# Both squared-ReLU MLPs of a two-layer decoder trunk, 29 of 32 weight tiles a layer multiplied by one level of Strassen's scheme

## The reference

```python
def mlp(h, w_up, w_down):                 # D_MODEL = 1024, D_FF = 4096
    u = jax.nn.relu(h @ w_up)
    return (u * u) @ w_down
# x = x + mlp(rmsnorm(x, w), w_up, w_down)   for each of the two layers
```

## Time and profile before

| | |
|---|---|
| median of three runs | 2374.9 us (2372.99 to 2383.7) |
| profiled execution, first to last instruction (span) | 2389.7 us |
| PE busy | 2199.2 us, 92% |
| DVE busy | 1364.9 us, 57% |
| ACT busy | 754.3 us, 32% |
| POOL busy | 396.1 us, 17% |
| MLP 0, MLP 1 | about 801 to 1186 us and 1984 to 2373 us |

### The profile page before, as it was taken

How to read it: one execution, slowest core, us unless ns; L and a number is a source line. 1 busy time by engine, 2 the same in 40 slices (tenths; PEclk the granted TensorE clock), 3 DMA queues, 4 the chain that set the end, 5 groups by cost and what they waited for, 6 DMA issues and landing times.

```text
span 2389.7 us, 41891 instructions
## 1 busy us (share of the span) xinstructions
PE 2199.2 (92%) x17594; PEld 2071.3 (87%) x17594; DVE 1364.9 (57%) x2086; ACT 754.3 (32%) x1439; POOL 396.1 (17%) x267
## 2 busy tenths in 40 slices
PE   7998897888899999999998998999899879999998
PEld 7988776777789999999998987897798759999997
DVE  4886776856654635344565564664656647353443
ACT  4332334445443312122313322322332334122221
POOL 1000101101121100000045443244325500000000
PEclk9999998887999999999999999999999989999998
DMA  4225676762333777787658778568757945877874
GB/s 166 71 70 176 234 253 232 272 226 92 102 122 134 263 269 254 262 270 257 233 179 278 242 231 294 171 205 292 242 174 257 327 161 198 276 264 247 280 248 178
DMA packets 282912, 519.95 MB, mean 218 GB/s; under 512 B 17777, under 2 KB 253665, under 8 KB 278881
## 3 DMA queue, kind: packets, MB, share of 16 engines
q1 hardware_dynamic: 271408, 324.44, 41.9%
q10 hardware_dynamic: 5888, 177.91, 20.5%
q0 software_dynamic: 5440, 15.08, 1.8%
HBM read 483.76 MB, written 210.80 MB: 291 GB/s over the span
## 4 chain that ended last, share of the span: by engine, by line
PE 62%; DVE 12%; issue 9%; DMA 9%; ACT 4%; POOL 3%; SPq 1%; ACTq 0%; DVEq 0%; POOLq 0%
PE gp L2352 33%; PE gp L2932 14%; DMA uk<-in_dil_k 3%; PE gp L2504 3%; PE gp L2714 3%; DMA vs<-in_dil_v 2%; DVE cacc L1601 2%; DMA decay<-tmp_a_row 2%; POOL uq L3038 2%; PE mp L2807 2%; PE mp L2882 1%; POOL at_f L2998 1%; ACT w_hi L1029 1%; DVE sc_t L2170 1%; PE mp L2775 1%
## 5 line engine op out<-in xcount | busy, mean ns | idle before, releaser
L2932 PE MATMUL gp<-a_hi,w_hi 128*128 128x272 f32 x1152 | 349.2, 304 | 2.1 <-DVE q_t L2096 2.0
L2932 PE MATMUL gp<-a_lo,w_hi 128*128 128x272 f32 x1152 | 333.7, 291 | 0.0
L2932 PE MATMUL gp<-a_hi,w_lo 128*128 128x272 f32 x1152 | 332.4, 290 | 0.0
L2352 PE MATMUL gp<-a_hi,w_hi 128*128 128x272 f32 x1456 | 306.9, 292 | 23.5 <-DVE w_lo L1524 12.2
L3038 POOL TENSOR_TENSOR uq<-uq,uk 128x1024 f32<-128x1024 f32 x96 | 262.5, 2738 | 287.0 <-DMA uk<-in_dil_k 286.8
L2352 PE MATMUL gp<-a_hi,w_lo 128*128 128x272 f32 x1456 | 302.8, 290 | 0.0
L2352 PE MATMUL gp<-a_lo,w_hi 128*128 128x272 f32 x1456 | 302.2, 289 | 0.0
L2352 PEld LDWEIGHTS gp<-a_hi,w_hi 128*128 128x128 f32 x1456 | 231.0, 190 | 26.2 <-DVE cin L1590 13.0
L2932 PEld LDWEIGHTS gp<-a_hi,w_hi 128*128 128x128 f32 x1152 | 218.6, 190 | 26.1 <-issue 22.6
L2352 PEld LDWEIGHTS gp<-a_hi,w_lo 128*128 128x128 f32 x1456 | 231.1, 190 | 0.0
L2352 PEld LDWEIGHTS gp<-a_lo,w_hi 128*128 128x128 f32 x1456 | 229.8, 190 | 0.0
(11 more groups left out here) (397 smaller groups left out, 4174.3 us busy)
## 6 DMA issues: line engine op xcount, KB each, us to landing
out_dil_ks<-in_dil_k ACTq DMA_DIRECT2D x32, 2044.0 KB
out_dil_vs<-in_dil_v ACTq DMA_DIRECT2D x32, 2044.0 KB
uq<-tmp_rows SPq DMA_DIRECT2D x96, 512.0 KB, 6.2
w_raw<-in_odd_w_in SPq DMA_DIRECT2D x36, 1024.0 KB, 8.3
vs<-in_dil_v SPq DMA_DIRECT2D x67, 512.0 KB, 7.2
w_raw<-in_w_up SPq DMA_DIRECT2D x32, 1024.0 KB, 8.2
w_raw<-in_w_down SPq DMA_DIRECT2D x32, 1024.0 KB, 7.9
uk<-in_dil_k SPq DMA_DIRECT2D x64, 512.0 KB, 7.2
```

Source lines behind the costliest of these rows:

```text
L2352: m = nc.tensor.matmul(gp[:, c, h, 0:HALF], w[:, sl, k, c * P:(c + 1) * P], x[:, k, h * HALF:(h + 1) * HALF], start=n < 2, stop=n >= 46)
L2932: m = nc.tensor.matmul(out, w[:, k, n * P:(n + 1) * P], x[:, k, h * HALF:(h + 1) * HALF], start=k == 0 and j == 0, stop=k == last_k and j ...
```

## The change: one level of Strassen's scheme (Winograd's form) for 29 tiles of 32

The first three tiles of a layer stay as they were (`MLP_STD = 3`). For the other 29 the tile is taken as a 2 x 2 block matrix, blocks being (even or odd row chunks) x (first or second 128 columns), each four 128x128 blocks; the operand is 2 x 2 as well, (even or odd feature chunks) x (token halves). Seven products of such blocks, each 4 x 3 = 12 matmuls, stand for the eight: 84 matmuls for 96. For this, sums have to be made:

- of the weights, four of 512 elements for each tile, in place in `w_raw`, on POOL (`unit_sums`);
- of the operand, three for each of the four pairs of chunks (544, 272 and 272 elements), once for each new operand, on POOL (`token_sums`), except for the fourth pair of each turn's hidden part, of which DVE makes the first;
- of the results, on DVE (`first_sums`, `second_sums`, `last_sums`), with copies out of PSUM on ACT.

Each tile is split in four pieces (512, 1024, 1024, 1024 elements, 3584 for 2048 before), since seven blocks are split and not four; each operand part in four pieces (272, 544, 544, 544 for each pair of chunks, 1904 for 1088). `w_hi` and `w_lo` become a ring of four half slots with a further small buffer for the seventh block. Two sets of four PSUM banks are used in turn (`gp`, `mp`). The loops over turns are written out. POOL's table DMAs for layer 1 move behind MLP 0, and ACT waits for the stored rows (`rows_stored`) before, and not after, the first chunks of MLP 1's operand are rounded.

```diff
+MLP_STD = 3
+MLP_N = 32
+def home(m, i):
+    return (3 * (m - MLP_STD) + 2 + i) % 4
...
 # SyncE: loads
+                for m in range(MLP_N):
...
+                    sp.wait_ge(w_lo_done, G - 1)
+                    sp.dma_start(w_raw[:, m % 2], src).then_inc(w_loaded[m % 2], 16)
...
 # ScalarE
+                def high2(m):
+                    act.wait_ge(s_sum, 1 + 4 * fast(lay, m) + 2)
+                    act.wait_ge(mm_done, chunks_before(base + m - 1) + 1)
+                    nc.scalar.activation(w_hi_q[:, home(m, 1)], raw_unit(m % 2, 1), ACT.Copy).then_inc(s_hi, 1)
+                def high3(m):
+                    act.wait_ge(s_sum, 1 + 4 * fast(lay, m) + 4)
...
+                        act.wait_ge(p_mm, 1 + 5 * fast(lay, m) - 2)
+                    nc.scalar.activation(w_hi_q[:, home(m, 2)], raw_unit(m % 2, 0), ACT.Copy).then_inc(w_hi_done, 1)
+                def hidden(j, i):
+                    t = h_raw[i % 2]
+                    act.wait_ge(drained, chunks_before(base + 8 * j + i) + 2)
+                    if j:
+                        st.link(nc.scalar.activation(t, t, ACT.Relu))
+                    if 8 * j + i + 1 >= MLP_STD:
+                        copy_third((8 * j + i + 1) // 8, i + 1)
+                    nc.scalar.activation(t, t, ACT.Square).then_inc(hid, 1)
...
+            rows_stored(act)
             for n in range(KC):
                 high_part(3, n)
...
-            rows_stored(act)
...
 # VectorE
+                def low_unit(m, i):
+                    q = home(m, i)
+                    return nc.vector.tensor_tensor(w_lo_q[:, q], raw_unit(m % 2, i % 2), w_hi_q[:, q].bitcast(F32), ALU.subtract)
+                def low_part_of(which, p, x, n, t, at):
+                    dve.wait_ge(part_hi_done[p], at)
+                    nc.vector.tensor_tensor(part_lo[which, p][:, x:x + n], t.rearrange("p (x n) -> p x n", x=n),
+                                            part_hi[which, p][:, x:x + n].bitcast(F32), ALU.subtract).then_inc(part_ready[p], 1)
...
+                for m in range(MLP_STD, MLP_N):
+                    j, u, n = m // 8, m % 8, m + 1
...
+                        last_sums(m - 1)
+                    if u == 4:
...
+                        last_hidden(j, HALF, 4 * HALF)
+                        last_hidden_sum(j)
+                        low_b2("b", 3, h_raw[1], parts_at(lay, j))
+                        low_t13("b", 3, h_raw[0], parts_at(lay, j))
+                        low22(n)
+                        low3(m)
+                        first_sums(m)
+                        low_t42("b", 3, h_raw[0], parts_at(lay, j))
+                        second_sums(m)
+                        low1(n)
+                        low2(n)
+                        low3(n)
+                        continue
+                    if n < MLP_N:
+                        low22(n)
+                        low1(n)
+                    if u in (2, 3) and m > MLP_STD:
+                        hidden_low_t(j, u - 2)
+                    first_sums(m)
...
+                    if 0 < u < 4:
+                        hidden_low(j, u - 1)
...
+                    second_sums(m)
...
+                    if n < MLP_N:
+                        low2(n)
+                    if u == 3:
+                        hidden_low_t(j, 2)
+                    elif n < MLP_N:
+                        low3(n)
...
 # TensorE
+            def fast_group(lay, m):
...
+                        for n, (w, v) in enumerate(((w_h, x_h), (w_l, x_h), (w_h, x_l))):
+                            z = nc.tensor.matmul(B[:, bank], w, v, start=(p == 0 and n == 0 and not more), stop=(p == 3 and n == 2),
+                                                 skip_group_check=True)
...
+                pe.wait_ge(drained, chunks_before(G - 1))
+                pe.wait_ge(s_lo, 3 * q + 2)
+                for ps in (((0, 1), (2,), (3,)) if u == 4 else ((0, 1, 2, 3),)):
+                    times(0, u1, 0, 0, 1, p_mm, ps)
+                    times(1, u1, 1, 1, 2, mm_done, ps)
+                    if ps[0] == 0:
+                        pe.wait_ge(s_lo, 3 * q + 3)
+                    times(2, u2, 1, 3, 3, p_mm, ps)
+                    times(3, u2, 0, 4, 3, p_mm, ps)
+                pe.wait_ge(w_lo_done, G + 1)
+                pe.wait_ge(snap, 1 + 2 * q + 1)
+                times(0, u3, 0, 6, 4, p_mm, more=True)
+                pe.wait_ge(snap, 1 + 2 * q + 2)
+                times(2, u3, 1, 2, 2, p_mm, more=True)
+                times(3, None, 0, 5, 4, mm_done, more=True)
...
 # GpSimd
-            pool.wait_ge(mm_done, 2 * G0["mlp0"])
+                def unit_sums(m, i):
+                    q, s = fast(lay, m), m % 2
+                    a11, a12, a21, a22 = (raw_part(s, k, f) for f in range(2) for k in range(2))
+                    if i == 0:
+                        pool.wait_ge(s_lo, 3 * q + 1)
+                        nc.gpsimd.tensor_tensor(a22, a21, a22, ALU.add).then_inc(s_sum, 1)
+                        nc.gpsimd.tensor_tensor(a21, a11, a21, ALU.subtract).then_inc(s_sum, 1)
+                        return
+                    pool.wait_ge(s_lo, 3 * q + 2)
+                    pool.wait_ge(s_sum, 1 + 4 * q + 2)
+                    nc.gpsimd.tensor_tensor(a11, a22, a11, ALU.subtract).then_inc(s_sum, 1)
+                    pool.wait_ge(s_sum, 1 + 4 * q + 3)
+                    nc.gpsimd.tensor_tensor(a12, a12, a11, ALU.subtract).then_inc(s_sum, 1)
...
+            mlp_sums(0)
+            pool.wait_ge(drained, 2 * G0["odd"])
             pool.dma_start(dists[:, 1], a["at_c"][:, 0:P]).then_inc(c1_in, 16)
...
-            pool.wait_ge(drained, 2 * G0["odd"])
```

More of the change, by code:

```diff
@@ L710, in build @@
         out_hw = sem("out_hw")
+        scaled, hid3, snap, p_mm, s_sum, s_hi, copied_out = so_done, so_rdy, a_row_done, so_mm, v_turned, so_hi, dt_parts
+        part_hi_done = [kt_done, smp_done, smt_done, root_sq]
+        part_ready = [smn_done, smf_done, c_h_done, sms_mm]
+        part_sum = [kt_mm, smt_mm, root_mm, c_h_mm]
         def wait(eng, s, v):
@@ L760, in rows_stored @@
             eng.wait_ge(v_stored[2], 64 * 4)
+            for g in range(3):
+                eng.wait_ge(k_stored[g], 16 * 4)
+            eng.wait_ge(vn_stored, 16 * 12)
             eng.wait_ge(row_stored, 16 * 24)
@@ new lines, in mlp @@
+                split_whole(1)
+                rms(1 + 2 * lay)
+                copy(0)
+                split_whole(2)
+                x_high(0)
+                hidden(0, 0)
+                x_high(1)
+                x_high_t(0)
+                hidden_high(0, 0)
+                copy(1)
+                high22(3)
+                high1(3)
+                x_high_t(1)
+                x_high(2)
+                hidden_high_t(0, 0)
+                hidden(0, 1)
+                x_high(3)
+                x_high_t(2)
@@ L1372, in _ @@
+                if lay == 0:
+                    next_half(1)
+                    next_half(0)
+                for c in range(2):
+                    final_parts(i_norm, 6 + c)
             mlp(0, 2)
@@ new lines, in next_half @@
+                def next_half(part):
+                    G, k = G0["odd"], slice(4 * part, 4 * part + 4)
+                    dve.wait_ge(s_hi if part else w_hi_done, 3 * MLP_FAST + 2 if part else G + 1)
+                    z = nc.vector.scalar_tensor_tensor(out=w_lo[:, 0, k], in0=w_raw[:, 0, k], scalar=HEAD_DIM ** -0.5,
+                                                       in1=w_hi[:, 0, k].bitcast(F32), op0=ALU.mult, op1=ALU.subtract)
+                    if part == 0:
+                        z.then_inc(w_lo_done, 1)
@@ L2045, in _ @@
+                if lay == 0:
+                    next_half(1)
+                    next_half(0)
+                last_sums(MLP_N - 1)
+                for c in range(2):
+                    final_parts(i_norm, 6 + c)
             mlp(0, 2)
@@ L2754, in _ @@
+            def mlp(lay, i_norm):
+                for m in range(MLP_N):
+                    if m < MLP_STD:
+                        group(f"mlp{lay}", 0, m, am_hi, am_lo, a_ready, AB[i_norm], sl=m % 2, norm=i_norm if m == 0 else None)
+                    else:
+                        fast_group(lay, m)
             mlp(0, 1)
```

462 lines of the change are left out of this document (367 added, 95 removed).

## The result

| | before | after |
|---|---|---|
| median | 2379.25 us, 4 runs (2372.99 to 2383.7) | 2546.18 us, 4 runs (2542.48 to 2555.07) |
| ratio | | 1.071, 95% interval 1.0685 to 1.0738 |
| span of the profiled execution | 2389.7 us | 2540.6 us |
| PE, DVE, ACT, POOL busy | 92, 57, 32, 17% | 86, 68, 38, 37% |

The change makes the kernel 7% slower; 2564 us (2435 to 2650) was predicted. The profiled executions differ by 150.9 us, and the loss lies in the two MLPs, where it was expected. By the first matmuls of the stretches: even layer before MLP 0 -9.3 us (first MLP matmul at 791.2 for 800.6), MLP 0 467.9 for 385.8, so +82.2, projection and attention of layer 1 794.4 for 797.4, so -2.9, MLP 1 and the end 487.0 for 406.0, so +81.0.

A forecast was written before the change was run, and what follows sets the result against it. GpSimd and two-SBUF-operand VectorE instructions exclude each other on one port, so the chain of sums and splits bounds the MLPs: 2 x (67.9 tiles + 26 start) + 1 table DMAs = 189 on 2374.9, 2564 us (2435 to 2650).

The forecast's parts named there:

- The light tile: Last three w_down tiles, first w_up tile of a turn: 12.8 us by chain, 11.8 if fourth sum gets in first.
- The fuller tiles: Second to fifth tile of a turn: 14.3, 15.7, 16.9, 16.8 us, counting only GpSimd and VectorE time on the port.
- The start: Three plain tiles before the fast loop: norm wait plus port work, 62.1 us against 36.1, so +26 a layer.
- rival 3: Clock gives way, partly to 1.2 GHz, in most of the fuller tiles: +63 us, 2627 and above; chance 0.07.
- (b): Sign of being right: GpSimd's 512 sums average well above 1.4 us, VectorE's 1024 splits well above 1.23.
- (e): Sign of being right: TensorE waits for VectorE sums and `w_lo`.
- (c): Sign of being right: a light tile at 12 to 13 us, a turn of eight at about 115 against 96.
- (a): Sign of being right: fast matmuls at 125 ns spacing, but TensorE busy some 75% of each MLP.
- (d): Sign of being right: a gap of some 20 us or more before tile 3.
- rival 1: The port packs well, sums get in between and chains overlap across tiles: +90 to +130 us, 2480; chance 0.16.
- rival 2: Exclusion is not the bound, GpSimd's chain runs as if alone: light tile 10.9 us, total -37, 2338; chance 0.15.
- rival 4: Near cancelling: packing so good that starts and tiles give back the 87 us, 2375; chance 0.04.

The follow-up runs named there:

- experiment 1: Changed kernel with every GpSimd sum cut to 8 elements a partition, waits, splits and matmuls kept: 2385.4 us, 1.005 of the kernel before.
- experiment 2: Changed kernel with each GpSimd sum replaced by two fills of its target, which read nothing from SBUF: 2393.3 us, 1.008 of the kernel before.
- experiment 6: Changed kernel with only GpSimd's weight sums cut to 8 elements, operand sums kept: 2468.5 us, 1.037 of the kernel before.
- experiment 8: Kernel with fast tiles in w_down only, with a third seventh-block buffer, a fifth ring quarter and pieces made earlier: 2401.0 us, 1.0096 of the kernel before.
- experiment 9: Kernel of experiment 8 with four steps reordered in the first and last fast tiles: 2406.0 us, 1.010 of the kernel before.
- experiment 10: Kernel of experiment 9 with 12 and 8 useless matmuls filling TensorE's waits in the first fast tile: 2397.9 us, 1.008 of the kernel before.
- experiment 11: Kernel of experiment 10 with the second fast tile's third split and the next one moved behind its first sums: 2400.4 us, 1.010 of the kernel before.
- experiment 12: Kernel of experiment 11 with that order (splits behind the tile's own first sums) in all last three fast tiles: 2362.9 us, 0.993 of the kernel before.
- experiment 5: Changed kernel with only GpSimd's operand sums cut to 8 elements, weight sums kept: 2503.1 us, 1.052 of the kernel before.

## Why the prediction was right, and where its steps were off

*TensorE's part* (-87.2 us, 10.53 us a tile): right. Wherever nothing else held it, a fast tile took 10.5 (experiments 1, 2, 6 and 8 to 12). But this gain reached the end only where the chain ran through TensorE.

*The exclusion* as what bounds: shown, by experiment 2 (153 of 161 us, with the reserve named there). Free sums took 1.3 where 1.37 was put, standing ones 2.2.

*The light tile*, 12.8: it took 11.8, the number given for the case that the fourth sum gets in first. That was not the reason. The split did stand first, and the fourth sum stood for it, but each of the two standing sums stood 0.9 us where 1.2 was put, and each of the four sums was itself 0.1 shorter. The kind of bound was right, which experiment 8 confirms: with the chain cut, the same work passes in 10.5. Over 15 tiles the term was 16.9 us too large, of which 4.5 lie in MLP 0's very last tile, which has no next tile's pieces beside it (8.3 us).

*The fuller tiles*: predicted 14.3, 15.7, 16.9 and 16.8; measured, as means over MLP 0's full turns, 13.1, 18.3, 19.3 and 17.1. The fifth was right, the second 1.2 too large, the third and fourth 2.6 and 2.4 too small. The step that failed for these two is "Here the port has more work, so I count port time alone". The port alone is not what sets them: with next to no GpSimd work they still take 13.2 and 14.3 (experiment 1), so that the order of copies, squares, roundings and splits across VectorE and ScalarE is a chain of its own, and with either kind of sum they go to 17 and 18 (5, 6). In MLP 0 the three third tiles came to 7.9 us more than put, the three full fourth ones to 7.3 more, tile 3 to 3.4 less (13.5), the second ones to 3.7 less, the fifth ones to 1.1 more and the light ones to 16.9 less, with 0.9 behind the last sums; the loop comes out at 410.0 for 416.8 because these cancel in part. That is luck.

*The start*: 62.1 put, 58.0 measured to the first piece of tile 4. Its place was wrong: tile 3 begins at 828.5, with hardly a gap behind the plain tiles, and the time is lost inside it; its matmuls take 33.3 us, with waits of 4.6, 3.0 and 7.3 us among them.

*The table DMAs*: +1 put, nothing seen; the stretch between the MLPs is 2.9 us shorter.

*The clock*: the forecast charged nothing and rival 3 63 us. In MLP 0's chain of waits the 420 fast matmuls took 73.5 us, where 125.3 ns each would be 52.6: 20.9 us of the layer's 82.2 are slow matmuls on the path, and in MLP 1's it is 21.0 (540 matmuls, 88.7 for 67.7). Of the 20.9 some 18 lie in the second, third and fourth tiles of the turns, 1.6 to 2.8 us in each, and 2.3 in tile 3; at 936.3 to 939.5, in a second tile, the granted clock is 0.50, in the light tile above 1.00. In the third and fourth tiles it is about what they took beyond the forecast; how much of that the clock alone makes was not separated. Without it the forecast's chain was too expensive by about 33 us in MLP 0 (11.7 + 20.9).

*What the sum did not have*: MLP 0 begins 9.3 us earlier than before. In the profiled executions of the twelve kernels of the experiments it began between 786.5 and 795.3, so the 800.6 of the kernel before may be one execution's; it was not followed up and stays open.

Sum: -11.7 and -12.9 in the two MLPs, -9.3 ahead of them, -3.9 between them: 151 instead of 189 on the profiled executions. So the direction and the cause were right, and that the total came so near is in part luck: a chain priced too high in the light tiles and at the start stood against third and fourth tiles and a clock that were priced too low.

*Signs*: (b) and (e) were as described, and (c) but for a light tile just under 12; (a) in part, with 82% of busy time for 75, most of the difference being half clock; (d) was in the wrong place. Of the signs of being wrong one did appear, the half clock in the fuller tiles: 288 of MLP 0's 2436 fast matmuls start 0.20 to 0.24 us behind the one before. *Rivals*: rival 1 (2480) falls, since the light tiles' chains do not overlap (11.8 and not 10.5) and a turn took 115 us and not under 100; rival 2 (2338) falls with experiment 2; rival 3's mechanism is there, at two thirds of its price (20.9 + 21.0 for 63); rival 4 would have needed full tiles of 12.

## What to carry to other kernels

Fewer matmuls pay only where the chain of waits is TensorE's before and after; what makes them possible (sums, splits) has to be priced as a chain through the in-order queues, not as load, tile by tile. Give it to tiles whose neighbours have room, and keep what TensorE waits for (draining and first sums) ahead of what it needs only later; a wait cured in one tile reappears in the next while the same order stands there. Sums that read SBUF on GpSimd and two-operand VectorE work add up instead of running side by side: here the one that came second stood, 0.9 us a time in a light tile.
